# Narrow products of a decoder step spread over the array's four 32-column groups

## The reference, cut to what matters

```python
mod = silu(c) @ w_ada + b_ada                      # c: 1 prompt row + 8 sample rows; w_ada: 1024 x 6144
sh1, sc1, g1, sh2, sc2, g2 = split(mod, 6)
xn  = rms_norm(x, norm1_g) * (1 + sc1) + sh1
qa, ka, va, qb, kb, vb, iq, ik, iw = split_proj(xn @ w_in)       # w_in: 1024 x 2888
# q and k: rms_norm per head, rotary.  An indexer (iq, ik, iw) picks the top keys of mixer B
oa = dilated window attention, 8 heads             # samples: 256 window rows + the new ones, per sequence
ob = attention over the picked keys, 8 heads       # samples: 2 cache pages of 128 rows + the new ones
x  = x + g1 * (concat(oa, ob) @ w_out)
xn = rms_norm(x, norm2_g) * (1 + sc2) + sh2
y  = x + g2 * ((silu(xn @ w_gate) * (xn @ w_up)) @ w_down)
```

## Time and profile before

| | |
|---|---|
| time, median of 3 executions | 1975.32 us (1973.96 to 1977.28) |
| span of the profiled execution | 1973.0 us |
| PE matmul busy | 1793.4 us (91%) |
| DVE busy | 943.3 us (48%) |
| ACT busy | 666.8 us (34%) |
| POOL busy | 533.4 us (27%) |
| DMA | 135.37 MB, mean 69 GB/s |

### The profile page before, as it was taken

The page is one execution under the profiler, slowest core; times in us unless marked ns, Lnnn a source line. Parts: engine busy times, 40 slices in busy tenths (PEclk is TensorE's granted clock), DMA queues, the critical chain, the costliest instruction groups (busy, mean ns, idle before and its releaser), DMA issues. The chain is left out here.

```text
span 1973.0 us, 30833 instructions
## 1 busy us (share of the span) xinstructions
PE 1793.4 (91%) x11234; PEld 1617.2 (82%) x11234; DVE 943.3 (48%) x2221; ACT 666.8 (34%) x1784; POOL 533.4 (27%) x661
## 2 busy tenths in 40 slices
PE   6797779899975999999788998999999999999998
PEld 4495368787864888888536988999999999999998
DVE  2705698897893777777523134331232133133124
ACT  4415323321413888888312224112111111111211
POOL 0235234440543221210201204223313222222310
PEclk8898789999986999999898999999999999999999
DMA  6600013334204121110235112111112111111002
GB/s 228 227 22 14 14 33 120 126 113 139 95 18 137 54 85 56 52 42 1 83 117 184 33 43 65 38 49 43 43 43 64 43 32 53 43 43 43 21 1 88
DMA packets 137907, 135.37 MB, mean 69 GB/s; under 512 B 7085, under 2 KB 126813, under 8 KB 137158
## 3 DMA queue, kind: packets, MB, share of 16 engines
q1 hardware_dynamic: 136150, 131.07, 21.0%
q0 software_dynamic: 1648, 2.89, 0.5%
HBM read 115.29 MB, written 27.04 MB: 72 GB/s over the span
## 5 line engine op out<-in xcount | busy, mean ns | idle before, releaser
L2417 DVE TENSOR_TENSOR hf<-bank,sg 128x352 f32<-128x352 f32 x66 | 34.6, 525 | 464.4 <-PE bank L2165 455.2
L2165 PE MATMUL bank<-ahi,gwh 128*128 128x352 f32 x1056 | 196.4, 328 | 11.2 <-DVE hf L2417 6.6
L2326 POOL TENSOR_TENSOR hlo<-hf,hhi 128x352 fp32r<-128x352 f32 x66 | 62.5, 946 | 504.8 <-ACT hhi L2255 504.8
L2430 DVE SCALAR_TENSOR_TENSOR x<-wide,modT,x 128x352 f32<-128x352 f32 (+1 forms) x264 | 151.2, 573 | 97.1 <-PE wide L2181 97.1
L2165 PE MATMUL bank<-alo,gwh 128*128 128x352 f32 x1056 | 192.2, 324 | 2.0 <-DVE alo L2406 2.0
L2165 PE MATMUL bank<-ahi,gwl 128*128 128x352 f32 x1056 | 193.9, 326 | 0.0
L2165 PEld LDWEIGHTS bank<-ahi,gwh 128*128 128x128 f32 x1056 | 176.3, 190 | 14.0 <-DVE hf L2417 6.9
L1164 DVE TENSOR_SCALAR_CACHE_REDUCE junk<-sig,cand 128x896 uint8<-128x896 f32 (+6 forms) x217 | 177.9, 877 | 0.6
L2165 PEld LDWEIGHTS bank<-alo,gwh 128*128 128x128 f32 x1056 | 174.3, 189 | 2.7 <-DVE alo L2406 2.7
L2165 PEld LDWEIGHTS bank<-ahi,gwl 128*128 128x128 f32 x1056 | 176.4, 191 | 0.0
L1526 PE MATMUL bank<-diag,prob 128*128 128x128 f32 x1152 | 167.3, 282 | 5.3 <-ACT diag L1662 4.1
(11 more groups left out here) (298 smaller groups left out, 3489.0 us busy)
## 6 DMA issues: line engine op xcount, KB each, us to landing
raw<-in_w_ada SPq DMA_DIRECT2D x24, 1024.0 KB, 5.5
gw<-in_w_gate_up SPq DMA_DIRECT2D x44, 512.0 KB, 5.2
raw<-in_w_in SPq DMA_DIRECT2D x11, 1024.0 KB, 5.4
dw<-in_w_down SPq DMA_DIRECT2D x22, 512.0 KB, 3.5
scr_x<-xT SPq DMA_DIRECT2D x1, 4224.0 KB, 16.1
xnat<-in_x_prompt SPq DMA_DIRECT2D x8, 512.0 KB, 5.3
scr_q<-ubuf SPq DMA_DIRECT2D x32, 128.0 KB
qn<-scr_q SPq DMA_DIRECT2D x8, 512.0 KB, 4.0
```

The lines of the kernel that those rows point to most:

```text
L2165: mm = pe.matmul(pb[2 * s + side][:, 0:THIRD], a[r][:, k, side, :], b[:, k, third(th)], start=(p == 0 and k == 0), stop=(p == 2 and k == K ...
L2326: pool.tensor_tensor(hlo[:, r, third(th)], hf[:, (3 * r + th) % 2, :], hhi[:, r, third(th)].bitcast(F32), ALU.subtract).then_inc(h_lo, 1)
L2417: v.tensor_tensor(hf[:, s, :], pb[2 * s + 1][:, 0:THIRD], sg[:, s, :], ALU.mult).then_inc(h_mul, 1)
L2430: ins = v.scalar_tensor_tensor(out=x1[:, d, cols], in0=src[:, 0:n], scalar=modT[:, 40 + d, 0:1], in1=x1[:, d, cols], op0=ALU.mult, op1=ALU ...
```

## The change: what it does, and the diff

`cT` is padded with zeros to 32 columns. The eight products of a modulation chunk go to partitions 0, 32, 64, 96 of the bank in turn, two per group of 32, so the bank holds four partial sums in 128 rows. ACT copies all 128 rows. The two transposes become two ordinary f32 products with `fold` (128 x 9, made once by DVE from the identity), which turn the rows and add the four partial sums. In sample attention `kTa` and `kTb` get a buffer for each of the 8 sequences, the copies no longer wait for scores, the scores of four sequences are made together (`scores(g)`: head pair outside, sequence inside), sequences 0 to 3 after the transposes of sequence 4, sequences 4 to 7 at the end. The value products of four sequences alternate in the same way. The new keys are copied by two broadcast copies in place of four. `ob` shares its place with `kw`.

```diff
-    cT = T.at("cT", [P, KD, 9], F32, T.end)
+    cT = T.at("cT", [P, KD, 32], F32, T.end)
...
-    modn = T.at("modn", [9, 2, WCH], F32, T.end)
+    modn = T.at("modn", [P, 2, WCH], F32, T.end)
+    fold = T.at("fold", [P, 32], F32, T.end)
...
                 for k in range(KD):
-                    mm = pe.matmul(ada_bank[a][0][0:9, 0:WCH], cT[:, k, :], raw[:, n % 3, k, :],
-                                   start=(k == 0), stop=(k == KD - 1))
+                    rows = slice(32 * (k % 4), 32 * (k % 4) + 32)
+                    mm = pe.matmul(ada_bank[a][0][rows, 0:WCH], cT[:, k, :], raw[:, n % 3, k, :],
+                                   start=(k < 4), stop=(k >= 4))
...
-                    mm = pe.transpose(ada_bank[a][1][:, j * 9:j * 9 + 9], modn[:, a % 2, j * P:(j + 1) * P],
-                                      ident[0:9, 0:9])
+                    mm = pe.matmul(ada_bank[a][1][:, j * 9:j * 9 + 9], modn[:, a % 2, j * P:(j + 1) * P],
+                                   fold[:, 0:9], start=True, stop=True)
...
-                act.activation(modn[:, a % 2, :], ada_bank[a][0][0:9, 0:WCH], ACT.Copy).then_inc(ada_nat, 1)
+                act.activation(modn[:, a % 2, :], ada_bank[a][0][:, 0:WCH], ACT.Copy).then_inc(ada_nat, 1)
...
+            v.memset(cT[:], 0.0).then_inc(c_zero, 1)
+            v.wait_ge(ident_in, 16)
+            v.tensor_reduce(fold[:], ident[:].rearrange("p (g n) -> p n g", g=4), AX.X, ALU.add)
+            v.wait_ge(c_zero, 1)
...
+            def scores(g):
+                pe.wait_ge(ke, 3 + 2 * (4 * g + 3))
+                pe.wait_ge(ke_a, 4 * g + 4)
+                for c in range(4):
+                    for n4 in range(4):
+                        n, r = 4 * g + n4, 32 * n4
+                        pe.matmul(wide[g][r:r + 32, 0:NEWW], qa[:, c, n].rearrange("p h t -> p (h t)"),
+                                  kTa[:, n, c, :], start=(c == 0), stop=(c == 3))
+                for n4 in range(4):
+                    n, r = 4 * g + n4, 32 * n4
+                    mm = pe.matmul(wide[g][r:r + 32, 512:512 + NEWW], qb[:, n].rearrange("p h t -> p (h t)"),
+                                   kTb[:, n, :], start=True, stop=True)
+                mm.then_inc(sc, 4)
...
-                pe.wait_ge(ke, 3 + 2 * n)
-                pe.wait_ge(ke_a, n + 1)
-                for c in range(4):
-                    pe.matmul(wide[g][r:r + 32, 0:NEWW], qa[:, c, n].rearrange("p h t -> p (h t)"),
-                              kTa[:, n % 2, c, :], start=(c == 0), stop=(c == 3))
-                pe.matmul(wide[g][r:r + 32, 512:512 + NEWW], qb[:, n].rearrange("p h t -> p (h t)"),
-                          kTb[:, n % 2, :], start=True, stop=True).then_inc(sc, 1)
+                if n == 4:
+                    scores(0)
+            scores(1)
...
-                for n4 in range(4):
-                    n, r = 4 * g + n4, 32 * n4
-                    for a in range(3):
-                        w = P if a < 2 else NSAMP
+                for a in range(3):
+                    w = P if a < 2 else NSAMP
+                    for n4 in range(4):
+                        n, r = 4 * g + n4, 32 * n4
...
-                if n >= 2:
-                    act.wait_ge(sc, n - 1)
-                act.activation(kTa[:, n % 2, :, P:2 * P],
+                act.activation(kTa[:, n, :, P:2 * P],
...
-                if n >= 2:
-                    v.wait_ge(sc, n - 1)
-                v.tensor_copy(kTa[:, n % 2, :, 0:P],
+                v.tensor_copy(kTa[:, n, :, 0:P],
```

More of the change, by code:

```diff
@@ L131, in __init__ @@
         self.size = nc.sbuf_usable_end - self.base
+        self.top = 0
     def at(self, name, shape, dt, off):
@@ L135, in at @@
         self.end = off + (size + 31) // 32 * 32
+        self.top = max(self.top, self.end)
         assert self.end <= self.size, (name, self.end)
@@ L202, in front @@
     valid = T.at("valid", [NSAMP, NEWW], F32, T.end)
-    modn = T.at("modn", [9, 2, WCH], F32, T.end)
-    assert T.end <= 24576, T.end
-    XB = 24576
+    modn = T.at("modn", [P, 2, WCH], F32, T.end)
+    fold = T.at("fold", [P, 32], F32, T.end)
+    assert T.end <= 25344, T.end
+    XB = 25344
     xhi = T.at("xhi", [P, KD, 1152], F32R, XB)
@@ L348, in front @@
     small_t = sem("small_t")
+    c_zero = sem("c_zero")
     small_e = sem("small_e")
@@ L1012, in _ @@
                     v.wait_ge(small_t, 9)
-                    v.tensor_copy(cT[:].rearrange("p k n -> p (k n)"), bank[0][:, 0:72])
+                    v.tensor_copy(cT[:, :, 0:9], bank[0][:, 0:72].rearrange("p (k n) -> p k n", n=9))
                     v.tensor_copy(vecT[:], bank[1][:, 0:64]).then_inc(small_e, 1)
@@ L1750, in sample_attention @@
     qb = T.at("qb_blk", [P, NSEQ, 8, TSEQ], F32, T.end)
-    kw = T.at("kw", [P, 3, KT, 512], F32, T.end)
+    ob = T.at("ob_s", [P, 4, 512], F32, T.end)
+    kw = T.at("kw", [P, 3, KT, 512], F32, T.end - 8192)
     vw = T.at("vw", [P, NSEQ, KT, 512], F32, T.end)
     vpg = T.at("vpg", [P, NSEQ, KT, P], F32, T.end)
-    kTa = T.at("kTa", [P, 2, 4, NEWW], F32, T.end)
-    kTb = T.at("kTb", [P, 2, NEWW], F32, T.end)
+    kTa = T.at("kTa", [P, NSEQ, 4, NEWW], F32, T.end)
+    kTb = T.at("kTb", [P, NSEQ, NEWW], F32, T.end)
     expand = T.at("expand2", [NSAMP, 2, P], F32, T.end)
@@ L1762, in sample_attention @@
     pT = T.at("pT_s", [P, 4, 3, P], F32, T.end)
-    ob = T.at("ob_s", [P, 4, 512], F32, T.end)
     nmax = T.at("nmax_s", [P, 4], F32, T.end)
@@ L1767, in sample_attention @@
     n_pool = A["cache_k"].shape[1]
-    assert T.end <= S["loaded"]
+    assert T.end <= S["loaded"], (T.end, S["loaded"])
     ldc = sem("s_consts")
@@ L1844, in _ @@
             pe.wait_ge(kv_pg, 16 * KT * NSEQ)
+            def scores(g):
[11 more added lines that the diff above has]
+                mm.then_inc(sc, 4)
             for n in range(NSEQ):
-                g, r = n // 4, 32 * (n % 4)
                 pe.wait_ge(k_in[n % 3], 16 * (n // 3 + 1))
@@ L1933, in _ @@
             v.wait_ge(kt, 2)
[L1934 to L1937, removed]
+            v.tensor_copy(kTa[:, :, :, PAST:NEWW], bank[1][:, 0:128].rearrange("p (c n) -> p c n", c=4)
+                          .unsqueeze(1).to_broadcast([P, NSEQ, 4, NSAMP]))
+            v.tensor_copy(kTb[:, :, PAST:NEWW], bank[1][:, 128:160].unsqueeze(1).to_broadcast([P, NSEQ, NSAMP])
+                          ).then_inc(ke, 1)
             for g in range(2):
@@ L1942, in _ @@
                 v.wait_ge(kt, 3 + 3 * n)
-                if n >= 2:
-                    v.wait_ge(sc, n - 1)
-                v.tensor_copy(kTa[:, n % 2, :, 0:P],
+                v.tensor_copy(kTa[:, n, :, 0:P],
                               bank[2][:].rearrange("p (c n) -> p c n", c=4)).then_inc(ke, 1)
                 v.wait_ge(kt, 2 + 3 * (n + 1))
-                v.tensor_copy(kTb[:, n % 2, 0:PAST], bank[1][:, 0:PAST]).then_inc(ke, 1)
+                v.tensor_copy(kTb[:, n, 0:PAST], bank[1][:, 0:PAST]).then_inc(ke, 1)
             v.wait_ge(ldc, NCONST)
```

## The result

The changed kernel takes 1924.9 us (median of four executions, 1923.4 to 1927.1) against 1975.1 for the kernel before on the same chip: a ratio of 0.9744 (95% interval 0.973 to 0.9758), 50.2 us less. The forecast was 1942 with a range of 1923 to 1970. The time lies at the fast end of the range, outside the forecast's own range of 1933 to 1952 and at the rival "four groups at once" (1924), and that is also what the trace shows. The profiled execution has a span of 1923.1 us, 49.9 less than before.

What follows compares the result with a forecast made beforehand. PE was taken to bound the start and sample part, DVE the later pairs. Gains of 8.6 - 3 + 14.8 + 13.2 = 33.6 us took 1975.3 to 1941.7 us by the runs, range 1923 to 1970.

Steps and rivals of the forecast that it cites:

- four groups at once: Rival for start, pairs and samples: all four column groups run at once, 51.5 us gained, 1924 us; chance 0.17.
- the first one: Matmul streams: starts keep program order, a product costs one pitch, so eight products take 9 pitches in place of 16.
- the two bounds: Matmul streams: either a matmul costs its pitch as today, or all four column groups run together at a quarter.
- Start: Modulation chunks 0 to 7: 8.6 us gained, bounds 0 to 11.
- The chain to `xhi`: Chunks 0 to 7: weight loads landing after 6.5 us each, chunk 6 between; `xhi` starts at 63.9 against 72.48.
- Later pairs: Modulation chunks 8 to 23: PE waits for DVE in six of eight pairs; loss of 3 us, bounds +6 to -9.
- The price of the larger turn: Chunks 8 to 23: the turn's two extra matmuls, slow, cost 0.4 us six times, 2.4 us.
- Scores: Sample attention: four sequences' scores take 21 pitches, 5.0 us; 14.8 us gained, between 5.7 and 19.7.
- Values: Sample attention's value products: 31.1 us become 17.9, 13.2 gained, between 2.9 and 21.8.
- No overlap: Rival for all streams: matmuls in different column groups never run side by side; 6.2 us gained, 1969 us; chance 0.19.
- The fourth rival: DVE's list eats more: start's gain lost in the indexer's first wait, or all pairs slow; 10 us less, 1951; 0.10.
- every change of the column group empties the array: Rival for about 150 products changing groups: each change costs, 18 us at 0.12 each, 1987 us; chance 0.09.

Runs made afterwards that it cites:

- the third to the fifth experiment: Changed kernel with modulation products in blocks of four matmuls (1926.0 us); scores in blocks of eight (1933.4 us); modulation in two groups, blocks of eight (1937.1 us, profiled).
- `val_blocks`: Changed kernel with the sample values' sequence as outer loop, six matmuls in a row in one column group: 1948.5 us, ratio 0.9875.
- `sample_only`: Kernel before with the sample attention's part of the change alone, modulation as it was: 1936.8 us, ratio 0.9811.
- the eighth experiment: Changed kernel with the later pairs' chunks 8 to 23 kept in one column group, copy and turn of 32 rows: 1932.6 us, ratio 0.9787.
- experiments 6 and 7: Changed kernel with all value products in blocks per sequence (1948.5 us); with only 128-row products in blocks, 32-row products following for all four sequences (1927.1 us).
- the third experiment: Changed kernel with a modulation chunk's eight products in blocks (0,0,1,1,2,2,3,3) over the column groups instead of in turn: 1926.0 us, ratio 0.9757.
- `keep_warm`: Changed kernel with 50 useless matmuls ahead of the second turn of the six later pairs not behind va: 1919.3 us, ratio 0.9725.
- `before`: The kernel before, without any edit, run beside the experiments: 1973.1, 1973.7 and 1976.0 us on the three chips.

## Why the prediction came out as it did

**The step that failed is the first one.** "Starts keep the order of the program, so a product costs one pitch": they don't, across column groups. Each group keeps the order of its own matmuls, and the next group's start beside them as long as no more than four are held in a group (the third to the fifth experiment). A product's two passes are two of those four, so products in turn over four groups run four at once, 4 pitches for 16 matmuls where I took 9. I had the two bounds right and chose the value between them from the order of the stream, which no row of before could show for different groups. All that follows has this size in it: with the value for four at once the same sums gave 1924. That the time still lies in the stated range is owed to the range, which was drawn out to this rival, and not to the mechanism that was forecast.

By the terms:

- Start: forecast 8.6, measured 10.25 in the profiled runs, bound 11. Over all traces it is 77.35, 75.92 and 78.18 us with the old modulation, and 66.05 to 70.07 (mean of nine 68.5) with the new. The shape was as forecast: DVE's thirds and the weight loads become last, and PE's waits for them are where the rest of the faster stream goes. The chain to `xhi` had two loads of 6.5 us in it; they took 5.0 and 8.3, and chunk 6 between them took the 2 us that I gave it, but four at once at half clock (1.93). That costs nothing, as far as the runs can show: in `val_blocks` this chunk ran warm (1.07 us), and the load behind it landed 2.7 us behind the load before it there too, as it does here.
- Later pairs: forecast a loss of 3, within bounds of +6 to -9; measured a gain of 1.1, and over six traces with the new pairs (371.4 to 375.6) against two with the old ones (374.0 and 375.4) no difference that can be told from their scatter. The parts were the right ones: the two pairs behind va gained (first bias to second bias 4.30 us in both before, 1.00 and 2.11 after), the fourth pair turned cold as said (chain 4.20 to 6.15), the seventh too (5.02 to 7.21, though `sample_only`, with the old pairs, already has 6.52 there). PE's waits were forecast at 38 us and are 45.9, since the streams became shorter than I took them. The price of the larger turn, 2.4 in my sum, was too low: DVE's waits for it alone grew by 19.7 - 15.1 = 4.6 us in the eighth experiment.
- Scores: forecast 14.8, four at once 19.7, measured 17.8. A group of 40 matmuls takes 2.6 us as the four-way case has it. The ring of three key loads takes part of it back: PE waits 1.20 and 0.76 us for `kw`. I had taken 3.5 us for such a load, as in the kernel before; now that the transposes run ahead it takes 4.9 (median of the eight).
- Values: forecast 13.2, four at once 21.8, measured 21.6. That it comes so near to 21.8 is partly chance: with the same products the other traces give 19.5 to 23.6, by the clock that was granted. The cold first result (3.64 us) was in the sum. Not in it was the next step, which here runs partly cold (5.67 us against 4.39). Of the eight other traces with the faster values only two repeat that (5.24 and 5.48 us); in the other six it took 3.75.

No overlap is refuted by the 1.07 us of a chunk. The fourth rival was partly right: the six pairs that wait for DVE all had a granted clock of 0.58 to 0.71 in their chains, but the two behind va kept 0.96 and more, and nothing of the start's gain was lost in the indexer (-0.2 us). The rival "every change of the column group empties the array" is refuted in every stretch. Its mechanism exists, but hangs on the change of the row count and not of the group (experiments 6 and 7). This agrees with the Trainium skill, "TensorEngine Tiling (Array Packing)", Key Properties: a change of the tiling mode, unlike one of the tile alone, drains the engine.

The rank of the rivals is what I would change. I gave four at once 0.17, and its only counter-argument was two passes per product. The Trainium skill, "TensorE: Matmul & The Clock Gate", Part 3, says that matmuls start and end in strict order. I had used it for the forecast; the third experiment disagrees, with 1.10 us for 16 matmuls in blocks of four where strict order makes 13 pitches, 2.8 us. The same section's measured ratio, 2.38 for three column tiles, was the better guide: here it is 3.61 / 1.07 = 3.4 for four.

## What to carry to other kernels

Matmuls with at most 32 weight columns are worth spreading over the four column groups, in turn or in blocks of at most four matmuls (two f32 products), and the number of weight rows must not change inside the loop over the groups. Before a stream is made shorter, look who waits at its end: the samples, where PE was last, gave three quarters of the gain, and the later pairs, where PE waited for DVE, gave none until the wait itself was moved, by a second bank. A longer wait can leave the work behind it at the half clock (1.00 to 0.67 behind the fourth pair), and here it did so in some executions and not in others, so price that work at both levels. And look which loads had time to spare before: the values' loads had 6.9 us and now have 0.2.

## What the runs showed of the hardware that was not expected

- Column groups take matmuls out of the list's order: four groups at once with 7 ns between their starts is what 1.07 us for 16 matmuls of 256 columns comes from; each group holds four, a fifth stops what is behind it (5.6 us for 40 matmuls in blocks of eight, 2.6 in turn; 2.78 us for 16 in two blocks of eight). The number four is read from these starts, for f32 products of two passes only.
- Across a change between 128 and 32 weight rows nothing runs side by side, though the groups differ: 2.81 us a sequence in `val_blocks`, with no overlap at all.
- The clock can fall although PE was kept busy until 1.6 us before the turn: 0.74 behind the third pair in `keep_warm`, 1.00 behind the second and the fourth. Nor does the same code after the same wait of 2.03 us always get the same clock: 1.00 in `before`, 0.72 in `sample_only`. What decides it was not found.
